# A hybrid attention, convolution and gated-MLP layer in float32: down-projection by seven block products, layer norm and output-weight splits beside the last head groups

## The chip, the cores and the metric

The kernel runs on one core of a Trainium2 chip. The time is the device time of one execution in microseconds (us). A core has five engines that run their own instruction streams and wait for each other by semaphores: TensorE (PE; PEld is its weight load), VectorE (DVE), ScalarE (ACT), GpSimd (POOL) and SyncE (SP), which here only starts transfers (DMAs).

## The reference, cut to what matters

```python
mod = silu(c) @ w_mod + b_mod                      # sh1, sc1, g1, sh2, sc2, g2
h = modulate(rms_norm(x, norm_mix_w), sh1, sc1)
proj = h @ w_in                                    # q, k, v, and the two GLU halves
attn_out = windowed_gqa_with_context(...)          # 8 query heads in 2 groups, window 128, 256 context keys
u = depthwise_conv(ga * sigmoid(gb), conv_w, conv_b)              # 31 taps, 512 channels
u = silu(layer_norm(u, conv_norm_w, conv_norm_b))                 # over the 512 channels
x = x + g1 * (concatenate([attn_out, u]) @ w_out)
h2 = modulate(rms_norm(x, norm_ffn_w), sh2, sc2)
up = depthwise_conv(h2 @ w_up, ffn_conv_w, ffn_conv_b)            # 3 taps, 2 x 2816 channels
x = x + g2 * ((silu(gate) * val) @ w_down)                        # 2816 -> 1024
```

There are 1024 latent tokens, 256 context tokens and 1024 model channels. All is float32.

## The kernel before

Products of float32 accuracy are made from three products: each operand is split into a rounded high part (ScalarE copies it to the type fp32r) and a low part (VectorE subtracts the high part), and TensorE adds high by high, high by low and low by high.

The program has two blocks. The first ends with the attention, in 16 *head groups* (`NGRP`): group n takes 128 query tokens (`i = n // 2`) and one key-value group. For each group TensorE makes scores, turns the probabilities and multiplies by the values (L639); VectorE takes the maxima (L1111, L1114) and normalises (L1187 to L1194); ScalarE takes the exponentials (L859) and moves the turned probabilities (L909). Beside groups 9 to 14 runs the layer norm of the convolution's output `cacc` (`beside(n)` on each engine): means (groups 9, 10) and variances (11, 12, L654) by matmul, the root by ScalarE, the reciprocal of `rstd` over 128x1024 by VectorE (13, 14, L1140), the scaling by GpSimd (L474). After the last group follow, one behind the other: the column sums of the second modulation (L725), its rows (L730), the SiLU of `cacc` (L928), its high and low parts (L934, L1204), and, in the second block, the splits of the eight tiles of `w_out` (L1553, L1691) before the output projection (L1440) can start. Then come the residual, the second norm and the turn of `h2`.

The up-projection (L1470) has 22 hidden tiles j of 128 channels. Each is done by a Strassen-Winograd scheme with seven block products instead of eight, in the order 1, 6, 5, 7, 2, 3, 4, twelve matmuls each. For each tile VectorE makes four sums of weight blocks (`w_sums`, L1762), seven low parts (`split_low`, L1744), five sums of products (`add`, L1833), four side taps of the convolution (`side`, L1840, L1844) and one product gate by value (L1900). The hidden tile goes to memory (`hid_scratch`).

The down-projection (L1517 to L1519) is direct: two halves of the output columns, for each half 22 hidden tiles as steps. A step is 8 token tiles by 3 matmuls, into eight accumulator banks; the operands are split per step by `down_high` and `down_low`. `drain` multiplies a half's banks by the gate `g2b` (L1915); the residual is added by GpSimd (L1944, L1951) and by VectorE (L1919). Twenty hidden tiles are loaded back from memory at the start of this stage, in six transfers (`reload`).

## Time and profile before

| | us |
|---|---|
| median of 3 runs (lowest, highest) | 1262.68 (1261.58, 1265.69) |
| the profiled execution | 1265.57 |
| its span, first to last instruction | 1263.8 |
| granted TensorE clock, mean over the span | 0.968 of full |
| TensorE busy | 1185.3 (94%) |
| VectorE busy | 882.7 (70%) |
| ScalarE busy | 523.3 (41%) |
| GpSimd busy | 131.2 (10%) |

The durations come from the profiled execution; it took 1265.57 us, 2.9 us more than the median and within the spread of the runs. Matmuls overlap, so the pace of TensorE is read from long unbroken runs, not from the duration of one.

### The profile page before, as it was taken

To read this page: it belongs to the slowest core of one execution; us is meant where nothing else is said; L and a number is where in the kernel's file an instruction comes from. 1 tells how busy PE (TensorE), PEld (TensorE's weight loads), DVE (VectorE), ACT (ScalarE), POOL (GpSimd) and SP (SyncE) were. 2 spreads that over 40 slices of the span, in tenths; PEclk is the share of its full clock that TensorE was granted. 3 is DMA by queue.
4 is the path that set the end of the run, shared out by engine and by line. 5 is a ranking of instruction groups with operands and counts; after the bars stand their busy time and mean duration, and the time that the engine had idled before them with its cause. 6 is when DMAs were issued, how large, how long until landed. Compare 5 with 4: busy or idle time off the path is not lost.

```text
span 1263.8 us, 16827 instructions
## 1 busy us (share of the span) xinstructions
PE 1185.3 (94%) x5917; PEld 979.6 (78%) x5917; DVE 882.7 (70%) x1325; ACT 523.3 (41%) x876; POOL 131.2 (10%) x140
## 2 busy tenths in 40 slices
PE   5799999898999879997899999999999999999998
PEld 1378888798978867775688888888888878887887
DVE  0479988689864634356899988888888864456445
ACT  4452356855555653544454444454454321111110
POOL 2100111044552020000000000000000000013001
PEclk9899999989999959998899999999999999999999
DMA  9222555439998005212213322322323273222112
GB/s 380 94 71 88 115 111 114 121 79 262 255 264 209 2 1 171 112 51 67 83 53 99 100 70 80 100 65 84 100 61 105 107 284 135 98 67 92 50 50 83
DMA packets 91014, 143.04 MB, mean 113 GB/s; under 512 B 7114, under 2 KB 60482, under 8 KB 89940
## 3 DMA queue, kind: packets, MB, share of 16 engines
q1 hardware_dynamic: 80292, 104.43, 24.5%
q0 software_dynamic: 9520, 33.75, 12.8%
q10 hardware_dynamic: 1152, 4.19, 0.8%
q8 instruction: 31, 0.51, 0.2%
q14 instruction: 19, 0.16, 0.0%
HBM read 96.22 MB, written 18.87 MB: 91 GB/s over the span
## 4 chain that ended last, share of the span: by engine, by line
PE 53%; DVE 5%; ACT 3%; issue 1%; DMA 1%; DVEq 0%; ACTq 0%
PE ps L1470 31%; PE ps L1517 6%; PE ps L1518 6%; PE ps L1519 6%; PE ps L1440 4%; DMA dn_raw<-in_w_down 1%; ACT h_second L1570 1%; DVE xt L1702 1%; DVE gm L1699 1%; PE ps L1451 1%; ACT gm L1557 0%; ACT h_first L1570 0%; DVE w_op L1744 0%; DVE t_sum L1733 0%; ACT hx L1574 0%
## 5 line engine op out<-in xcount | busy, mean ns | idle before, releaser
L1470 PE MATMUL ps<-t_op,w_op 128*128 128x512 f32 x1056 | 249.4, 392 | 5.8 <-DVE cv L1833 4.7
L1470 PEld LDWEIGHTS ps<-t_op,w_op 128*128 128x128 f32 x1056 | 199.6, 189 | 49.1 <-issue 4.8
L1470 PE MATMUL ps<-hx,w_op 128*128 128x512 f32 x792 | 188.9, 392 | 4.1 <-DVE p_first L1705 3.2
L1470 PEld LDWEIGHTS ps<-hx,w_op 128*128 128x128 f32 x792 | 149.5, 189 | 36.5 <-DVE p_first L1705 3.6
L1577 ACT ACTIVATE w_op<-w_raw 128x512 fp32r<-128x512 f32 x130 | 79.2, 626 | 193.2 <-DVE w_raw L1762 148.4
L1517 PE MATMUL ps<-dnh,ah 128*128 128x512 f32 x352 | 137.3, 390 | 1.3 <-DVE al L1854 1.3
L1518 PE MATMUL ps<-dnl,ah 128*128 128x512 f32 x352 | 137.0, 389 | 0.0
L1519 PE MATMUL ps<-dnh,al 128*128 128x512 f32 x352 | 137.0, 389 | 0.0
L1671 ACT ACTIVATE dnh<-dn_raw 128x512 fp32r<-128x512 f32 x44 | 27.7, 633 | 203.4 <-PE ps L1519 186.0
L1850 DVE TENSOR_SCALAR ah<-hid 128x1024 fp32r (+1 forms) x44 | 31.6, 717 | 101.0 <-PE ps L1519 101.0
L639 PE MATMUL ps<-vraw,pt 128*128 128x64 f32 x608 | 84.4, 287 | 15.8 <-ACT pt L909 15.8
L1744 DVE TENSOR_TENSOR w_op<-w_raw,w_op 128x512 fp32r<-128x512 f32 x132 | 88.9, 688 | 14.2 <-ACT w_op L1577 13.3
L639 PEld LDWEIGHTS ps<-vraw,pt 128*128 128x128 f32 x608 | 80.8, 207 | 20.8 <-ACT pt L909 10.9
L1517 PEld LDWEIGHTS ps<-dnh,ah 128*128 128x128 f32 x352 | 66.1, 188 | 16.3 <-DVE al L1854 2.6
L1440 PE MATMUL ps<-woh,hx 128*128 128x512 f32 x256 | 73.4, 404 | 5.0 <-DVE wol L1691 5.0
L1519 PEld LDWEIGHTS ps<-dnh,al 128*128 128x128 f32 x352 | 66.1, 188 | 13.9
L1518 PEld LDWEIGHTS ps<-dnl,ah 128*128 128x128 f32 x352 | 66.1, 188 | 13.5
L1111 DVE TENSOR_REDUCE scal<-ps 128x1 f32<-128x640 f32 (+1 forms) x64 | 50.2, 785 | 32.9 <-PE ps L612 27.9
L1939 POOL DMA_DIRECT2D x<-x_scratch x1 | 1.0, 1025 | 614.2 <-PE ps L1519 614.2
L859 ACT ACTIVATE p<-ps,scal,msq 128x640 f32<-128x640 f32 (+1 forms) x60 | 51.8, 863 | 26.1 <-DVE scal L1114 23.9
L1440 PEld LDWEIGHTS ps<-woh,hx 128*128 128x128 f32 x256 | 49.0, 195 | 15.6 <-DVE wol L1691 5.3
L909 ACT ACTIVATE pt<-ps 128x512 f32<-128x512 f32 x76 | 44.9, 593 | 37.1 <-PE ps L627 37.1
(265 smaller groups left out, 2228.4 us busy)
## 6 DMA issues: line engine op xcount, KB each, us to landing
w_raw<-in_w_up SPq DMA_DIRECT2D x44, 512.0 KB, 4.7
wm<-in_w_mod SPq DMA_DIRECT2D x32, 512.0 KB, 6.5
...
dn_raw<-in_w_down SPq DMA_DIRECT2D x44, 256.0 KB, 2.8
...
hid<-hid_scratch SPq DMA_DIRECT2D x4, 2048.0 KB, 12.2
...
```

The costliest lines, as they stand in the source:

```text
L639: last = pe.matmul(ps[:, 6, hl * HD:(hl + 1) * HD], pt[:, it % NPT, hl * P:(hl + 1) * P], vraw[:, kts[j], g, :], start=(j == 0 and hl == 0 ...
L859: act.activation(probs(n)[:, hl, 0:w], score_ap(hh, w), ACT.Exp, scale=msq[:, CT + n // NG, GQ * (n % NG) + hl:GQ * (n % NG) + hl + 1], bi ...
L909: act.activation(pt[:, it % NPT, :], ps[:, 4 + it % 2, :], ACT.Copy).then_inc(pt_out, 1)
L1111: dve.reduce_max(s[:, 0, hl:hl + 1], score_ap(hh, w), axis=AX.X, negate=True).then_inc(max_done, 1)
L1440: last = pe.matmul(ps[:, b + hh, :], a, (woh, wol)[lo][:, k, hh * HALF:(hh + 1) * HALF], start=(k == 0 and v == 0 and lo == 0), stop=(k == ...
L1470: last = pe.matmul(bank_of(p, s), w_op[p][w][:, k, :], rows_of(p, k, v), start=(start and k == 0 and w == 0 and v == 0), stop=(k == KH - 1 ...
L1517: pe.matmul(ps[:, t, :], ah[b][:, 0, c_], dnh[b][:], start=(kind == "first"), stop=False)
L1518: pe.matmul(ps[:, t, :], ah[b][:, 0, c_], dnl[b][:], start=False, stop=False)
L1519: return pe.matmul(ps[:, t, :], al[b][:, 0, c_], dnh[b][:], start=False, stop=(kind == "last"))
L1577: act.activation(w_op[p][0][:], w_part(s, p), ACT.Copy).then_inc(up_hi, 1)
L1744: dve.tensor_tensor(out=w_op[p][1][:], in0=w_part(s, p), in1=f(w_op[p][0][:]), op=ALU.subtract).then_inc(up_lo, 1)
L1850: dve.tensor_scalar(ah[b][:], hid[:, bass.ds(k, 1), :], 1.0, None, ALU.mult).then_inc(dn_split, 1)
```

## The change

The down-projection uses the same seven-product scheme, over blocks of 512 tokens, 512 output columns and pairs of hidden tiles. There are 77 steps (7 products by 11 pairs), each of 4 token tiles by 3 matmuls. The hidden tiles are combined in place by VectorE (`down_sum`, 44 instructions of 128x512). The combined weights are made by GpSimd while the up-projection runs: 22 chunks, each with two loads, four subtractions of 128x256 and two stores to a scratch tensor `w_down_sums`, each step waiting for the one before. Hidden tiles are loaded back one by one, at most three at a time. Operand sets are three instead of two or three, raw weight buffers four instead of two. The four output quarters are finished at different times: VectorE reads the banks (`read_quad`, 20 instructions, and 8 at the end), GpSimd multiplies by the gate and adds the residual for three quarters and prepares the fourth (28 additions or products of 128x512). The fourth quarter's last additions, on VectorE, wait for all 28.

For the layer norm, the variances come out one per token in a column (group 11), root and reciprocal are taken on 8 columns, and matmuls with a diagonal matrix (groups 13, 14) spread them; VectorE scales `cacc` from the accumulator. The SiLU runs on ScalarE inside group 15, the column sums on TensorE inside group 15, and four of the eight splits of `w_out` beside groups 13 to 15. The other four alternate with the splits of `cacc` at the start of the second block, while the projection already runs.

In the diff the pieces stand in the order layer norm (SyncE, GpSimd, TensorE, ScalarE, VectorE), then down-projection (tables, SyncE, TensorE, ScalarE, VectorE, GpSimd).

```diff
-        rstd = at(73, "rstd", [P, T])
+        diag = at(73, "diag", [P, TT, P])
+        r_ln = rst[:, 0:TT]
...
+        def wo_split_high(act, k):
+            act.wait_ge(wo_in[k % 4], 16 * (k // 4 + 1))
+            if k < KT - 1:
+                act.activation(wo_op[k][0][:].rearrange("p b n -> p (b n)"), wo_raw[:, k % 4, :], ACT.Copy).then_inc(wo_hi, 1)
...
+        def wo_split_low(dve, k):
...
+        WO_AT = {13: (0,), 14: (1, 2), 15: (3,)}
...
+                for k in range(4, KT):
+                    sp.wait_ge(wo_lo, k - 3)
+                    sp.dma_start(wo_raw[:, k % 4, :], w_out[0, k * P:(k + 1) * P, :]).then_inc(wo_in[k % 4], 16)
...
-                pool.wait_ge(rec5, 4)
-                for ct in range(CTL):
-                    pool.tensor_tensor(out=cacc[:, ct, :], in0=cacc[:, ct, :], in1=rstd[:], op=ALU.mult).then_inc(scaled, 1)
...
+                    elif n == LN + 2:
+                        pe.wait_ge(ln_act, 2 * CTL)
+                        for b in range(TT):
+                            for ct in range(CTL):
+                                last = pe.matmul(ps[:, 7, b:b + 1], sqc[ct][:, b * P:(b + 1) * P], meanw[:, 0:1], start=(ct == 0), stop=(ct == CTL - 1))
+                        last.then_inc(ln_mm, 1)
+                    elif n in (LN + 4, LN + 5):
+                        pe.wait_ge(ln_dve, 11)
+                        q = slice((n - LN - 4) * TT // 2, (n - LN - 3) * TT // 2)
+                        pe.matmul(ps[:, 7, :], ones[:], diag[:, q, :].rearrange("p b n -> p (b n)"), start=True, stop=True).then_inc(ln_mm, 1)
+                    elif n == NGRP - 1:
+                        for c in range(2):
+                            pe.wait_ge(mod_acc[1 + c], 16 * KT)
+                            for j in range(KT):
+                                last = pe.matmul(ps[:, 7, c * KT + j:c * KT + j + 1], sums[1 + c][:, j * P:(j + 1) * P], ones[:, 0:1], start=True, stop=True)
+                        last.then_inc(col_mm, 1)
...
+                        if n == NGRP - 1 and j < CTL:
+                            act.wait_ge(ln_dve, 19)
+                            act.activation(cacc[:, j, :], cacc[:, j, :], ACT.Silu, scale=cols[:, C_CNW + j:C_CNW + j + 1],
+                                           bias=cols[:, C_CNB + j:C_CNB + j + 1]).then_inc(silu5, 1)
...
+                    elif n == LN + 3:
+                        dve.wait_ge(ln_act, 9)
+                        dve.reciprocal(r_ln, r_ln).then_inc(ln_dve, 1)
+                        dve.wait_ge(ln_dve, 10)
+                        dve.tensor_tensor(out=diag[:], in0=ident[:].unsqueeze(1).to_broadcast([P, TT, P]), in1=r_ln.unsqueeze(2).to_broadcast([P, TT, P]),
+                                          op=ALU.mult).then_inc(ln_dve, 1)
                     elif n in (LN + 4, LN + 5):
-                        for r in range(2):
-                            q = slice((2 * (n - LN - 4) + r) * CTX, (2 * (n - LN - 4) + r + 1) * CTX)
-                            if n == LN + 4:
-                                dve.wait_ge(sqrt5, 1)
-                            dve.reciprocal(rstd[:, q], rstd[:, q]).then_inc(rec5, 1)
+                        hh = n - LN - 4
+                        dve.wait_ge(ln_mm, 4 + hh)
+                        for ct in range(CTL):
+                            dve.tensor_tensor(out=cacc[:, ct, half(hh)], in0=cacc[:, ct, half(hh)], in1=ps[:, 7, :], op=ALU.mult).then_inc(ln_dve, 1)
...
+        NK2 = FT // 2
+        DOWN = (1, 6, 2, 5, 7, 3, 4)
+        NSTEP = len(DOWN) * NK2
+        UPPER = (1, 2, 7, 4)
...
+            def down_rows(p, i):
+                odd, even = hid[:, 2 * i + 1, :], hid[:, 2 * i, :]
+                return {1: odd[:, 0:HALF], 6: odd[:, 0:HALF], 2: even[:, 0:HALF], 5: odd[:, HALF:T], 7: odd[:, HALF:T],
+                        3: even[:, 0:HALF], 4: even[:, HALF:T]}[p]
...
+            RELOADS = (3, 2, 21, 20, 5, 4, 7, 6, 9, 8, 11, 10, 13, 12, 15, 14, 17, 16, 19, 18)
+            FREED = {5: 6, 9: 5, 13: 7, 17: 4}
...
+                def load_step(n):
+                    p, i = down_at(n)
+                    if n >= 4:
+                        sp.wait_ge(dn_split, 2 * (n - 4) + 2)
...
+                    sp.dma_start(dn_raw[n % 4][:], src).then_inc(wo_in[n % 4], 16)
...
+                sp.wait_ge(wd_out, 32 * 2 * NK2)
...
+                for i in range(16):
+                    reload(i)
+                for i in range(16, 20):
+                    load_step(i - 12)
+                    reload(i)
+                for n in range(8, NSTEP):
+                    load_step(n)
...
+                def down_product(n, t):
+                    p, i = down_at(n)
+                    b, c_ = n % 3, slice(t * P, (t + 1) * P)
+                    o = ps[:, (4 if p in UPPER else 0) + t, :]
+                    start = i == 0 and p not in (2, 3, 4)
+                    pe.matmul(o, ah[b][:, c_], dnh[b][:], start=start, stop=False, skip_group_check=True)
+                    pe.matmul(o, ah[b][:, c_], dnl[b][:], start=False, stop=False, skip_group_check=True)
+                    return pe.matmul(o, al[b][:, c_], dnh[b][:], start=False, stop=(i == NK2 - 1), skip_group_check=True)
...
+                    act.activation(ah[n % 3][:], down_rows(p, i), ACT.Copy).then_inc(dn_hi, 1)
+                    raw_in(act, n)
+                    act.activation(dnh[n % 3][:], dn_raw[n % 4][:], ACT.Copy).then_inc(dn_hi, 1)
...
+                def down_low(n):
+                    for r, (hi, lo) in enumerate(((ah, al), (dnh, dnl))):
+                        dve.wait_ge(dn_hi, 2 * n + r + 1)
+                        src = dn_raw[n % 4][:] if r else down_rows(*down_at(n))
+                        dve.tensor_tensor(out=lo[n % 3][:], in0=src, in1=f(hi[n % 3][:]), op=ALU.subtract).then_inc(dn_split, 1)
...
+                for t in range(TT // 2):
+                    dve.wait_ge(bank_mm, t + 1)
...
+                    dve.tensor_tensor(out=gout[1][:, t, :], in0=ps[:, 4 + t, :], in1=g2b[:, 0:HALF], op=ALU.mult).then_inc(quad_read, 1)
+                    dve.wait_ge(quad_read, 20 + 2 * t + 1)
+                    dve.wait_ge(pool_step, POOL_STEPS)
+                    dve.tensor_tensor(out=gout[1][:, t, :], in0=gout[1][:, t, :], in1=p1_all[:, t, :], op=ALU.add).then_inc(quad_read, 1)
...
+                pool.wait_ge(t_lo, 4)
+                pool.wait_ge(t_sum_done, 4 * (TT // 2))
+                chunk = 0
+                for i in range(NK2):
+                    for c0 in range(0, HALF, CTX):
+                        if chunk:
+                            pool.wait_ge(wd_out, 32 * chunk)
+                        for r in range(2):
+                            k = tile_of(2 * i + 1 - r)
+                            src = w_down[0, k * P:(k + 1) * P, :].rearrange("p (g c) -> p g c", g=2)[:, :, c0:c0 + CTX]
+                            pool.dma_start(wd[r][:], src).then_inc(wd_in, 16)
+                        pool.wait_ge(wd_in, 32 * (chunk + 1))
+                        b11, b12, b21, b22 = wd[0][:, 0, :], wd[0][:, 1, :], wd[1][:, 0, :], wd[1][:, 1, :]
+                        for n, (o, a, b) in enumerate(((b11, b12, b11), (b12, b22, b12), (b22, b22, b11), (b21, b21, b22))):
+                            if chunk or n:
+                                pool.wait_ge(wd_step, 4 * chunk + n)
+                            pool.tensor_tensor(out=o, in0=a, in1=b, op=ALU.subtract).then_inc(wd_step, 1)
+                        pool.wait_ge(wd_step, 4 * chunk + 4)
+                        for r in range(2):
+                            pool.dma_start(wd_sum[2 * r:2 * r + 2, i, :, c0:c0 + CTX].rearrange("g p c -> p g c"), wd[r][:]).then_inc(wd_out, 16)
+                        chunk += 1
...
+                for t in range(TT // 2):
+                    pool.wait_ge(quad_read, 16 + t + 1)
+                    step(gout[0][:, t, :], gout[0][:, t, :], g2[1], ALU.mult)
+                    step(gout[0][:, t, :], gout[0][:, t, :], xq[0][:, t, :], ALU.add)
+                    store(t, 0, 1, gout[0][:, t, :])
+                pool.wait_ge(xq_in[1], 32)
+                for t in range(TT // 2):
+                    step(p1_all[:, t, :], u2_all[:, t, :], g2[0], ALU.mult)
+                    step(p1_all[:, t, :], p1_all[:, t, :], xq[1][:, t, :], ALU.add)
```

TensorE at the end of the head groups, before: behind the values of the last group (L639) stand the column sums (`ones,sums`, L725), the rows (L730), the turn of the last outputs (L649), then the projection (L1440).

```order
L639 MATMUL ps<-vraw,pt 128x64 x4
L627 MATMUL ps<-ident,p_103 128x128 x4
L649 MATMUL ps<-ident,on 128x128 x2
L639 MATMUL ps<-vraw,pt 128x64 x8
L725 MATMUL ps<-ones,sums_99 128x1 x8
L725 MATMUL ps<-ones,sums_100 128x1 x8
L730 MATMUL ps<-sums_98,ones 128x512 x2
L730 MATMUL ps<-sums_101,ones 128x512 x2
L649 MATMUL ps<-ident,on 128x128 x2
```

The same place now (L705 column sums, L669 values, L657 turned probabilities, L764 rows):

```order
L657 MATMUL ps<-ident,p_103 128x128 x8
L705 MATMUL ps<-ones,sums_99 128x1 x8
L705 MATMUL ps<-ones,sums_100 128x1 x8
L669 MATMUL ps<-vraw,pt 128x64 x4
L657 MATMUL ps<-ident,p_103 128x128 x4
L669 MATMUL ps<-vraw,pt 128x64 x4
L657 MATMUL ps<-ident,p_103 128x128 x4
L679 MATMUL ps<-ident,on 128x128 x2
L669 MATMUL ps<-vraw,pt 128x64 x8
L764 MATMUL ps<-sums_98,ones 128x512 x2
L764 MATMUL ps<-sums_101,ones 128x512 x2
L679 MATMUL ps<-ident,on 128x128 x2
```

The column sums have moved in front of the last group's values; only the rows and the turn of the last outputs still stand between the values and the projection.

ScalarE in group 15 and at the start of the second block, now (L950 moves probabilities, L966 is the SiLU, L305 and L308 split `w_out`, L1605 splits `cacc`, L1609 moves the gates' rows):

```order
L966 ACTIVATE cacc<-cacc,cols 128x1024
L950 ACTIVATE pt<-ps 128x512
L899 ACTIVATE hx<-ps 128x2x128
L966 ACTIVATE cacc<-cacc,cols 128x1024
L305 ACTIVATE wo_op_118<-wo_raw 128x1024
L344 UNCONDITIONAL_BRANCH
L1595 UNCONDITIONAL_BRANCH
L1600 ACTIVATE hx<-ps 128x2x128
L1605 ACTIVATE hx<-cacc 128x2x512
L305 ACTIVATE wo_op_120<-wo_raw 128x1024
L1605 ACTIVATE hx<-cacc 128x2x512
L305 ACTIVATE wo_op_122<-wo_raw 128x1024
```

Before, four SiLU, four splits of `cacc`, four moves of rows and then eight splits of `w_out` stood here in blocks behind the last group.

GpSimd during the up-projection, where nothing stood before (the scaling L474 was followed by the residual's load, L1939), now, one chunk of 22:

```order
L2066 DMA wd_5478<-in_w_down 128x2x256
L2066 DMA wd_5479<-in_w_down 128x2x256
L2072 TENSOR_TENSOR wd_5478<-wd_5478 128x256
L2072 TENSOR_TENSOR wd_5478<-wd_5479,wd_5478 128x256
L2072 TENSOR_TENSOR wd_5479<-wd_5479,wd_5478 128x256
L2072 TENSOR_TENSOR wd_5479<-wd_5479 128x256
L2075 DMA w_down_sums<-wd_5478 128x2x256
L2075 DMA w_down_sums<-wd_5479 128x2x256
```

All four subtractions have two inputs in SBUF. They run beside VectorE's work for the up-projection.

## Rows read from the trace of the kernel before

**Rows 1.** The page, part 1: busy time, share of the span, instructions

```profile
PE 1185.3 (94%) x5917; PEld 979.6 (78%) x5917; DVE 882.7 (70%) x1325; ACT 523.3 (41%) x876; POOL 131.2 (10%) x140
```

**Rows 2.** The chain of waits: start us, us, what

```profile
475.01 22.61 PE ps L1440 x90
...
634.43 381.11 PE ps L1470 x1680
...
1022.03 10.96 DMA dn_raw<-in_w_down
```

**Rows 3.** Busy time by stretch: stretch, length, engines, clock, DMA share, GB/s

```profile
450.00:475.00 25.00, 19.98 (x75) 16.12 (x73) 7.76 (x13) 16.29 (x20) 0.00 (x0) 0.57 0.00 1
634.00:1018.00 384.00, 383.73 (x1693) 317.63 (x1693) 334.50 (x442) 172.15 (x243) 0.00 (x0) 1.00 0.29 92
```

**Rows 4.** Instructions in order of time, TensorE: start us, us; in brackets idle before

```profile
441.68 1.97 PE L627 MATMUL ps<-ident,p 128*128 128x128 f32 x8 [1.81 <-ACT p L859]
447.80 1.94 PE L639 MATMUL ps<-vraw,pt 128*128 128x64 f32 x8 [4.14 <-ACT pt L909]
...
456.57 6.93 PE L725 MATMUL ps<-ones,sums 128*128 128x1 f32 x32
463.36 6.40 PE L730 MATMUL ps<-sums,ones 128*128 128x512 f32 x8
...
475.01 1.22 PE L1440 MATMUL ps<-woh,hx 128*128 128x512 f32 x2 [5.03 <-DVE wol L1691]
```

**Rows 5.** In order of time, VectorE, end of the head groups

```profile
436.52 3.35 DVE L1140 RECIPROCAL rstd<-rstd 128x256 f32<-128x256 f32 x2
...
442.28 2.35 DVE L1187 TENSOR_TENSOR scal<-scal 128x4 f32<-128x4 f32 x1
```

**Rows 6.** In order of time, GpSimd, end of the head groups

```profile
439.96 9.25 POOL L474 TENSOR_TENSOR cacc<-cacc,rstd 128x1024 f32<-128x1024 f32 x4 [43.05 <-DVE rstd L1140]
```

**Rows 7.** In order of time, ScalarE, behind the last head group

```profile
455.27 4.63 ACT L928 ACTIVATE cacc<-cacc,cols 128x1024 f32<-128x1024 f32 x4
```

**Rows 8.** In order of time, GpSimd, change of halves (second of eight alike)

```profile
1142.89 1.30 POOL L1944 TENSOR_TENSOR gout<-gout,x 128x512 f32<-128x512 f32 x1
```

**Rows 9.** In order of time, VectorE, change of halves

```profile
1139.88 0.68 DVE L1850 TENSOR_SCALAR ah<-hid 128x1024 fp32r<-128x1024 f32 x1
1140.48 2.09 DVE L1852 TENSOR_TENSOR dnl<-dn_raw,dnh 128x512 fp32r<-128x512 f32 x1
1142.49 2.79 DVE L1854 TENSOR_TENSOR al<-hid,ah 128x1024 fp32r<-128x1024 f32 x1
1145.21 1.77 DVE L1850 TENSOR_SCALAR ah<-hid 128x1024 fp32r<-128x1024 f32 x1
1146.91 2.27 DVE L1852 TENSOR_TENSOR dnl<-dn_raw,dnh 128x512 fp32r<-128x512 f32 x1
...
1151.86 0.69 DVE L1852 TENSOR_TENSOR dnl<-dn_raw,dnh 128x512 fp32r<-128x512 f32 x1
1152.47 1.22 DVE L1854 TENSOR_TENSOR al<-hid,ah 128x1024 fp32r<-128x1024 f32 x1
```

**Rows 10.** Who waited for whom, VectorE, 634 to 1010 us: total, times, longest

```profile
DVE w_op L1744 <- ACT w_op L1577: 13.3, 40, 0.7
DVE y L1840 <- ACT y L1657: 12.1, 20, 0.7
DVE u L1833 <- PE ps L1470: 8.9, 18, 0.7
```

**Rows 11.** In order of time, VectorE, inside one hidden tile

```profile
817.08 0.69 DVE L1833 TENSOR_TENSOR u<-ps,u 128x512 f32<-128x512 f32 x1 [0.59 <-PE ps L1470]
...
820.34 0.68 DVE L1833 TENSOR_TENSOR cv<-ps,u 128x512 f32<-128x512 f32 x1
```

**Rows 12.** The page, part 6: transfers, times, KB each, median us to landing

```profile
dn_raw<-in_w_down SPq DMA_DIRECT2D x44, 256.0 KB, 2.8
...
hid<-hid_scratch SPq DMA_DIRECT2D x4, 2048.0 KB, 12.2
```

**Rows 13.** In order of time, TensorE, first and last matmul of the down-projection

```profile
1018.09 0.39 PE L1517 MATMUL ps<-dnh,ah 128*128 128x512 f32 x1
...
1259.51 0.39 PE L1519 MATMUL ps<-dnh,al 128*128 128x512 f32 x1
```

541 lines of the change are left out of this document (298 added, 243 removed).

## The prediction

> **What bounds the kernel now.** I read the busy shares first, then the chain of waits, then busy time by stretch, then the waits of single engines.
>
> TensorE is busy for 94% of the span, VectorE for 70% [rows 1]. The share alone says that fewer matmuls should be worth their full price. The chain of waits says where: 1680 matmuls of the up-projection follow each other in 381.11 us without a break [rows 2], so TensorE's pace at the full clock is 381.11/1680 = 0.2268 us a matmul. In that same stretch VectorE is busy for 334.50 of 384.00 us, 87%, and GpSimd for nothing [rows 3]. That is the number to keep in mind: the stage is bound by TensorE, but VectorE is just behind it.
>
> The down-projection runs from 1018.09 to 1259.51 + 0.39 = 1259.9 us [rows 13], 241.8 us; its 1056 matmuls at 0.2268 us are 239.5, so 2.3 us are waits and starts. The rest of the span, to 1263.8, is a tail of 3.9 us.
>
> At the end of the head groups TensorE is not at its limit. It waits 1.81 and 4.14 us, then works through column sums and rows (6.93 and 6.40 us), then waits 5.03 us for the first split weights, and the projection starts at 475.01 [rows 4]. The granted clock between 450 and 475 is 0.57, so nearly all of it is at 1.2 GHz [rows 3]; it fell behind the two waits.
>
> **The change, part by part.** The sum is made against the profiled execution, 1265.6 us, which is 2.9 us above the median 1262.7. I subtract from both alike and give the time against the median.
>
> *Matmuls of the down-projection.* 77 steps x 12 = 924 instead of 1056. 132 x 0.2268 = 29.9 us less.
>
> *Start of that stage.* The steps are now 12 x 0.2268 = 2.72 us, half as long as before (24 matmuls, 5.44). VectorE's rest of the last hidden tile (side taps, gate product) covers steps 0 to 2, and splits of step 1 and of step 3 come about 1.4 and 0.9 us late: 2.5 us, as long as all waits there before (2.3). Hidden tiles: twenty of 512 KB. Before, 2048 KB landed in 12.2 us, and a weight load behind them took 10.96 us, to 1033, without a stop of TensorE [rows 12, 2]; as the reloads can't start before the last tile of the up-projection, at 1018.1 - 19.05 = 999, all 10,240 KB came in at most 34 us, 300 KB a us. With that the tiles needed by step 10 are there (by the 168 KB a us of a single transfer the last would be 15 us late); what is tight is the weights of step 4, which stand in SyncE's queue behind sixteen reloads. I take 0 for it and keep 9 us as the usual upper end.
>
> *Middle of that stage.* Per step VectorE does two low parts and at most one sum at 0.69 us [rows 9], 2.1 us and reads of banks, 2.3 of 2.72. It hides, as long as GpSimd leaves it alone.
>
> *End of that stage.* GpSimd's 28 instructions of 1.30 us [rows 8] plus about 0.3 between dependent ones. In the last product 8 of them wait for VectorE's reads at steps 1, 3, 5 and 7, the last at about 15.7 us, and 8 more follow: 15.7 + 4.1 + 8 x 1.6 + 5 for the port (below) = 37.6 us after that product's start, while TensorE needs 29.9 + 2.5 (VectorE's splits held up by those instructions) = 32.4. Then 7 VectorE instructions of 0.69 and a store of 2 us: the end is at about 45, where TensorE's end plus the old tail would be 33.8. That is 11 to 12 us lost, of which the tail is most. Together the down-projection gives 29.9 - 0.2 - 12 = 17.7; I take 18, range 8 to 24.
>
> *Layer norm and output weights.* Off the path behind the last group go: the column sums (6.93 us there, half of that at the full clock inside group 15), SiLU (4.63 us for four [rows 7]), the splits of `cacc`, and the wait of 5.03. What makes the 4.14 us wait goes too: GpSimd's scaling of 128x1024 (9.25 us for four [rows 6]) held a VectorE instruction on four elements for 2.35 us, and the two reciprocals before it took 3.35 [rows 5]; now four products of 0.69 us stand in their place. Added inside groups 13 to 15: two spreading matmuls (about 0.9 us each, by eight instructions of 128x512 at half clock in 6.40 us), four splits of 1.06 and 1.23 us, SiLU with its table between the moves of probabilities. The last values end, I estimate, at 449 instead of 456.6; the rows take 3.2 at full and 6.4 at half clock; first projection at about 454. That is 21 us earlier than 475.01. The first two token tiles take 22.61 us [rows 2] against 96 x 0.2268 = 21.8. The remaining splits (VectorE 2.5 us a tile, TensorE 2.72 a tile) keep ahead. I take 21 us, range 10 to 25.
>
> *GpSimd beside the up-projection.* This is the term that decides. A GpSimd subtraction of 128x512 takes 1.30 us [rows 8], one of 128x1024 9.25/4 = 2.31 [rows 6]; 1.01 us per 512 columns and 0.29 fixed, so 0.80 us for 128x256. What does it cost VectorE? At the change of halves four VectorE instructions took 2.09 + 2.79 + 1.77 + 2.27 = 8.92 us against 0.69 + 1.22 + 0.68 + 0.69 = 3.28 undisturbed [rows 9]: 5.64 us more, for four GpSimd instructions of 1.30 us, 1.08 times their length. The two engines take turns. Per hidden tile of 84 x 0.2268 = 19.05 us VectorE has 16 instructions with two SBUF inputs, 11 of 128x512 at 0.69 and 5 of 128x1024 at 1.22 [rows 9], 13.7 us or 0.72; those that read the accumulators are not held. So one subtraction costs 0.80 x 1.08 x 0.72 = 0.62 us and 88 of them 55 us. From this goes VectorE's slack. Its waits are 13.3, 12.1 and 8.9 us over twenty tiles [rows 10]; the 12.1 and a quarter of the 13.3 are its own chains through ScalarE and stay, the other 19 us are about 1.0 to 1.1 a tile. A chunk is two loads (3.4 us with 2.8 to landing [rows 12]), four subtractions with turns taken (6) and two stores (3.5), 13 us; 22 chunks last 286 us, 14 tiles, 15 us of slack. Once, a lead is used up: the sum `cv` is made at 820.34 to 821.0, and product 4 needs it three products of 2.72 us after 817.08 [rows 11], at 825.2, 4 us later. So TensorE loses 55 - 15 - 4 = 36 us. Bounds: no less than 0 (nothing VectorE does gets faster); with 0.80 x 1.08 = 0.86 us each, held every time, 76 - 19 = 57. I take 36.
>
> The Trainium skill (GPSIMD Engine Reference, section 3.1, "side-by-side cycle accounting") gives 4497 ns for a two-input addition of 2048 columns. Estimated from that page alone, 256 columns take 0.56 us, the term becomes 88 x 0.56 x 1.08 x 0.72 - 19 = 19 us and the whole time 1243. Rows 6 and 8 show a fixed part of 0.29 us on top, which such a short instruction pays in full, so I go by the rows.
>
> Sum: -18 - 21 + 36 = -3; 1262.7 - 3 = 1260 us (1262 to 1263 for a profiled execution like the one read here).
>
> **Rivals.**
> *B. The weight sums are nearly hidden.* If GpSimd mostly gets in while VectorE waits or reads accumulators, or its turns are short, one subtraction costs 0.3 us: 26 - 19 = 7. Time 1262.7 - 39 + 7 = 1231. For it: TensorE has leads of 4 us and more, and VectorE has waits in each tile. Against: rows 9, where no turn was cheap.
> *C. VectorE becomes the bound of the up-projection for good, and it is slower.* Each subtraction is held or holds for its full 0.86 us: 57. Time 1262.7 - 39 + 57 = 1281. It decides from (39 + 19)/88 = 0.66 us each, only 6% above my value. For it: the turn costs a running VectorE instruction too, and waits of TensorE of 2 us and more came before the fall of its clock [rows 4, 3]. The Trainium skill (GPSIMD Engine Reference, section 1) says that GpSimd's SBUF interfaces contend with VectorE instructions "in a 2-port perf mode or with two SBUF inputs", which is the same list. The trace agrees: the reads of accumulators beside GpSimd kept 0.69 us.
> *D. The head groups give back only half.* ScalarE's table load, SiLU and splits stand between the moves of probabilities that TensorE waits for; 10 instead of 21: 1270.
>
> **How the numbers follow.** Forecast 0.50, B 0.22, C 0.20, D 0.08. A measurement of this kernel tells about 0.3%, 3.8 us, from no change. Around 1260 with some 8 us either way, the forecast divides into 0.23 faster, 0.16 same, 0.11 slower. B adds 0.22 to faster; C and most of D (0.27) to slower, 0.01 to same. So faster 0.45, same 0.17, slower 0.38. The forecast's own range is 1249 to 1271. Both signs hold much of the chance, so the range must reach to B and to C: 1232 to 1284.
>
> **What would show it.** In the profile after: in the stretch of GpSimd's chunks the period of a hidden tile, 22 to 23 us in the forecast, 19.5 in B, over 24 in C; TensorE's waits there named VectorE's `cv` or `w_op`; VectorE's low parts at 1.5 us beside a subtraction and 0.69 otherwise; a subtraction of 128x256 at 0.80 us. First projection matmul at about 454 us (D: 465). First to last matmul of the down-projection about 215 us, and a tail of about 12 us with VectorE waiting for GpSimd. Wrong is the prediction if the up-projection keeps its 381 us per twenty tiles, or if the down-projection stops for hidden tiles or weights for more than 5 us.

## The result, and the profile after

The changed kernel takes 1246.13 us, median of 4 runs (1244.12 to 1248.26), beside 1262.86 us (1261.58 to 1265.69) for the kernel before: a ratio of 0.9882, 95% interval 0.9858 to 0.9907. It is 1.2% faster. The forecast was 1260 us, the range 1232 to 1284. The profiled execution took 1244.66 us, with a span of 1242.9; before it was 1265.57 and 1263.8.

Here the difference of the two spans is split at the first matmul of a stage. The output projection's start stands in [rows 4], the down-projection's in [rows 13]; the up-projection of the kernel before began at 582.4.

| us | before | after | difference | predicted |
|---|---|---|---|---|
| first matmul of the output projection | 475.0 | 462.0 | -13.0 | -21 |
| first matmul of the up-projection | 582.4 | 566.8 | -15.6 | (same term) |
| up-projection | 435.7 | 445.8 | +10.1 | +36 |
| down-projection, first to last matmul | 241.8 | 224.7 | -17.1 | -27 |
| tail behind it | 3.9 | 5.6 | +1.7 | +8 |
| span | 1263.8 | 1242.9 | -20.9 | -3 |

Two terms of the sum of -3 were somewhat too good (head groups -21 against -15.6, down-projection with its tail -18 against -15.4), and one was much too bad: +36 against +10.1. The spans differ by 20.9 us and the medians by 16.7: the two traces lie 4.2 us further apart, and the trace of before has a spell at the half clock of about that price that the other has not (below).

Busy time of the changed kernel (the line that answers to [rows 1]):

```profile
PE 1158.3 (93%) x5837; PEld 958.3 (77%) x5837; DVE 945.7 (76%) x1405; ACT 579.1 (47%) x991; POOL 317.0 (26%) x335
```

The stretches that answer to [rows 3], columns as there:

```profile
450.00:475.00 25.00, 24.35 (x97) 19.32 (x98) 11.89 (x15) 16.26 (x22) 0.00 (x0) 0.82 0.16 54
634.00:1012.00 378.00, 375.33 (x1646) 307.78 (x1645) 346.18 (x428) 159.73 (x233) 140.85 (x152) 1.00 0.45 145
```

TensorE made 1693 matmuls in 384 us before, 4.409 a us; now 1646 in 378, 4.354. Its clock is full (1.00) in both. Count the matmuls rather than the busy time: the 1.2% that is missing is short waits. By this pace a hidden tile of 84 matmuls takes 19.3 us, against 19.05 before, 22 to 23 in the forecast and 19.5 in rival B.

**The head groups.** TensorE in order of time, from group 9 on (the third row and those below answer to [rows 4]), with idle time before in brackets:

```profile
356.55 3.60 PE L689 MATMUL ps<-cacc,meanw 128*128 128x512 f32 x8
...
387.46 10.77 PE L695 MATMUL ps<-meanw,sqc 128*128 128x1 f32 x64
...
443.86 3.63 PE L705 MATMUL ps<-ones,sums 128*128 128x1 f32 x32
...
450.33 1.97 PE L669 MATMUL ps<-vraw,pt 128*128 128x64 f32 x8 [1.29 <-ACT pt L950]
...
453.37 3.52 PE L669 MATMUL ps<-vraw,pt 128*128 128x64 f32 x16
456.68 4.75 PE L764 MATMUL ps<-sums,ones 128*128 128x512 f32 x8
461.26 0.38 PE L679 MATMUL ps<-ident,on 128*128 128x128 f32 x2
461.97 19.32 PE L1483 MATMUL ps<-wo_op,hx 128*128 128x512 f32 x84 [0.32 <-PEq L344]
```

The waits of 4.14 and 5.03 us and the 6.93 us of column sums behind the last group are gone, as predicted. Yet the rows L764 begin at 456.68, where the column sums began at 456.57 before; the prediction had the last values end at 449. So nothing was won inside the groups, and the dearest new piece there is the second line: the variance is now made in columns, 32 products of one column each (two records a product). They take 10.77 us, and VectorE stands still behind them:

```profile
401.78 0.82 DVE L1142 TENSOR_REDUCE scal<-ps 128x1 f32<-128x640 f32 x1 [13.46 <-PE ps L642]
```

In the kernel before, the variance was two wide sets, and the means of group 9 stood here:

```profile
360.66 3.60 PE L654 MATMUL ps<-cacc,meanw 128*128 128x512 f32 x8
391.55 3.60 PE L654 MATMUL ps<-sqc,meanw 128*128 128x512 f32 x8
405.80 3.60 PE L654 MATMUL ps<-sqc,meanw 128*128 128x512 f32 x8
```

Two things follow. The columns themselves cost 3.6 us more than the 7.2 of the two sets; the rest of their price is the half clock that TensorE had behind them, to 407 (from 385 to 415 the mean granted clock is 0.72, before it was 1.00). And the changed kernel was already 4.1 us ahead in group 9, before anything that the change moved: between 310 and 320 us the granted clock was 0.76 before and 1.00 after, over the same instructions. Of the 13.0 us only about 9 belong to the change.

**The up-projection.** GpSimd's subtractions, least, middle and longest time in ns:

```profile
L2072 POOL TENSOR_TENSOR wd<-wd x44: 726/1034/1714, 598.2 to 909.5; 128x256 f32<-128x256 f32 x44
L2072 POOL TENSOR_TENSOR wd<-wd,wd x44: 732/1076/1715, 599.1 to 907.8; 128x256 f32<-128x256 f32 x44
```

The shortest took 0.73 us (I had 0.80 for an undisturbed one); the median is 1.03 to 1.08. So here GpSimd waits for its turn too. TensorE's longest waits from 565 us to the end, in total, times and longest:

```profile
PE ps L1568 <- DVE dnl L1928: 10.1, 4, 5.1
PE ps L1518 <- DVE cv L1910: 7.9, 7, 6.4
PE ps L1518 <- DVE p_first L1782: 4.2, 1, 4.2
PE ps L1518 <- DVE u L1910: 3.7, 4, 2.3
```

VectorE's own waits, 634 to 1005 us, answer to [rows 10]: the slack was spent first.

```profile
DVE w_op L1821 <- ACT w_op L1633: 6.9, 37, 0.5
DVE y L1917 <- ACT y L1713: 6.6, 14, 0.7
...
DVE u L1910 <- PE ps L1518: 1.2, 2, 0.7
```

**The down-projection.** First and last matmul (as [rows 13]), then the chain of waits into its fifth step:

```profile
1012.59 0.39 PE L1568 MATMUL ps<-dnh,ah 128*128 128x512 f32 x1
...
1236.93 0.39 PE L1570 MATMUL ps<-dnh,al 128*128 128x512 f32 x1
```

```profile
1014.86 8.11 DMA hid<-hid_scratch
1022.99 0.33 SPq L1450
1023.36 6.14 DMA dn_raw<-in_w_down
1029.53 0.64 ACT dnh L1735
1030.19 0.70 DVE dnl L1928
1030.94 0.80 PE ps L1568
```

The transfer of the weights of step 4 is issued at 1023.36, behind sixteen reloads, before which SyncE waits for earlier ones to land (at most three are on their way). It takes 6.14 us, against a median of 2.8 before [rows 12], and lands at 1029.50, and TensorE, which had waited 5.12 us, goes on at 1030.94. The eleven matmuls behind it come every 0.43 us instead of 0.23: the granted clock is at 1.2 GHz until 1035.6.

At the other end, VectorE beside GpSimd's last eight instructions (VectorE, then GpSimd):

```profile
1222.55 2.26 DVE L1928 TENSOR_TENSOR al<-hid,ah 128x512 fp32r<-128x512 f32 x1
1224.74 1.78 DVE L1928 TENSOR_TENSOR dnl<-dn_raw,dnh 128x512 fp32r<-128x512 f32 x1
1226.45 1.74 DVE L1928 TENSOR_TENSOR al<-hid,ah 128x512 fp32r<-128x512 f32 x1
1228.11 1.74 DVE L1928 TENSOR_TENSOR dnl<-dn_raw,dnh 128x512 fp32r<-128x512 f32 x1
...
1235.18 0.69 DVE L2052 TENSOR_TENSOR gout<-gout,p_all 128x512 f32<-128x512 f32 x1 [1.79 <-POOL p_all L2089]
```

```profile
1222.96 1.30 POOL L2089 TENSOR_TENSOR p_all<-u_all,g2b 128x512 f32<-128x512 f32 x1
...
1233.78 1.30 POOL L2089 TENSOR_TENSOR p_all<-p_all,xq 128x512 f32<-128x512 f32 x1
```

Low parts of 0.69 us take 1.74 to 2.26, and TensorE stands for 3.40 us before its last two steps (matmul at 1230.01).

### The profile page after: what moved, and what is told of

The parts are those of the page before. It is cut to its first block, busy times and chain, and to the rows that moved or that the text cites. A ratio compares the mean times of both kernels' runs of the same rounds, so it can differ in the third digit from the quotient of the medians.

```text
span 1242.9 us, 16857 instructions
## 1 busy us (share of the span) xinstructions
PE 1158.3 (93%) x5837; PEld 958.3 (77%) x5837; DVE 945.7 (76%) x1405; ACT 579.1 (47%) x991; POOL 317.0 (26%) x335
## 4 chain that ended last, share of the span: by engine, by line
PE 32%; DVE 15%; issue 6%; ACT 6%; DMA 3%; DVEq 0%; ACTq 0%; SPq 0%
PE ps L1518 13%; PE ps L1568 5%; PE ps L1569 5%; PE ps L1570 5%; PE ps L1483 3%; DVE w_op L1821 3%; DVE y L1921 3%; DMA hid<-hid_scratch 2%; DVE w_raw L1839 2%; ACT w_op L1633 1%; DVE y L1917 1%; ACT y L1713 1%; DVE u L1910 1%; DVE s_sum L1839 1%; ACT h_second L1626 1%
## 5 line engine op out<-in xcount | busy, mean ns | idle before, releaser
L1568 PE MATMUL ps<-dnh,ah 128*128 128x512 f32 x308 | 121.9, 396 | 10.1 <-DVE dnl L1928 10.1
L1569 PE MATMUL ps<-dnl,ah 128*128 128x512 f32 x308 | 121.5, 395 | 0.0
L1570 PE MATMUL ps<-dnh,al 128*128 128x512 f32 x308 | 121.3, 394 | 0.0
L1733 ACT ACTIVATE ah<-hid 128x512 fp32r<-128x512 f32 x77 | 48.6, 632 | 113.3 <-PE ps L1570 104.8
L2066 POOL DMA_DIRECT2D wd<-in_w_down x44 | 32.0, 729 | 271.8 <-DVE h_first L1810 199.3
L669 PE MATMUL ps<-vraw,pt 128*128 128x64 f32 x608 | 84.2, 287 | 8.9 <-ACT pt L950 8.9
L1928 DVE TENSOR_TENSOR al<-hid,ah 128x512 fp32r<-128x512 f32 x77 | 63.6, 826 | 36.0 <-ACT ah L1733 35.1
L669 PEld LDWEIGHTS ps<-vraw,pt 128*128 128x128 f32 x608 | 80.3, 206 | 13.6 <-ACT pt L950 10.6
L1483 PE MATMUL ps<-wo_op,hx 128*128 128x512 f32 x336 | 80.2, 395 | 0.3 <-PEq L344 0.3
L1483 PEld LDWEIGHTS ps<-wo_op,hx 128*128 128x128 f32 x336 | 62.9, 190 | 13.7 <-issue 0.5
L1928 DVE TENSOR_TENSOR dnl<-dn_raw,dnh 128x512 fp32r<-128x512 f32 x77 | 68.0, 884 | 6.4 <-ACT dnh L1735 6.2
L2072 POOL TENSOR_TENSOR wd<-wd 128x256 f32<-128x256 f32 x44 | 46.2, 1051 | 71.5 <-DMA wd<-in_w_down 69.8
```

The lines of the kernel that those rows point to most:

```text
L669: last = pe.matmul(ps[:, 6, hl * HD:(hl + 1) * HD], pt[:, it % NPT, hl * P:(hl + 1) * P], vraw[:, kts[j], g, :], start=(j == 0 and hl == 0 ...
L1483: last = pe.matmul(ps[:, b + hh, :], a, wo_half(k, lo, hh), start=(k == 0 and v == 0 and lo == 0), stop=(k == KT - 1 and v == 1))
L1568: pe.matmul(o, ah[b][:, c_], dnh[b][:], start=start, stop=False, skip_group_check=True)
L1569: pe.matmul(o, ah[b][:, c_], dnl[b][:], start=False, stop=False, skip_group_check=True)
L1570: return pe.matmul(o, al[b][:, c_], dnh[b][:], start=False, stop=(i == NK2 - 1), skip_group_check=True)
L1733: act.activation(ah[n % 3][:], down_rows(p, i), ACT.Copy).then_inc(dn_hi, 1)
```

## Experiments

All are edits of the changed kernel; each was run beside the kernel before, so ratios are the means of comparison. A stage's length is more exact than the whole time: the eight kernels with identical head groups begin their projection at 459.8 to 466.3 us, 72.8 to 78.7 us after the first product of the variance. Where nothing in them differs, the up-projection takes 444.3 to 446.7 us and the down-projection 224.2 to 227.9; its wait for the weights of step 4 is 5.1 to 8.6 us.

### 1 and 2. What costs the up-projection its 10 us

The first leaves out the subtractions:

```diff
-                        for n, (o, a, b) in enumerate(((b11, b12, b11), (b12, b22, b12), (b22, b22, b11), (b21, b21, b22))):
...
-                            pool.tensor_tensor(out=o, in0=a, in1=b, op=ALU.subtract).then_inc(wd_step, 1)
```

The second leaves out the whole loop over chunks, and the down-projection loads unchanged weights in their place:

```diff
-                        src = wd_sum[{5: 0, 7: 1, 4: 2, 6: 3}[p], i]
+                        src = w_down[0, k * P:(k + 1) * P, 0:HALF]
...
-                for i in range(NK2):
-                    for c0 in range(0, HALF, CTX):
...
```

> The changed kernel without GpSimd's four subtractions per chunk beside the up-projection; the chunks' loads and stores stay (the weights of four products are then not combined: the computation is incomplete). Theory (the turns that GpSimd and VectorE take at SBUF cost the whole loss of the up-projection): the stage, 445.8 us in the changed kernel, falls by 8 to 11 us to about 436, the 6.4 us stop of TensorE near 605 shrinks to 4 to 5, VectorE's low parts of weights go from 811 back to about 690 ns; time about 1236 us. Rival (the chunks' 88 transfers beside the stage's own are the cost): the stage stays above 443 us, time above 1243.

> The changed kernel without the chunks at all: neither loads, nor subtractions, nor stores beside the up-projection; the down-projection loads unchanged weights of the same size in their place (the computation is incomplete). Theory (turns of the two engines only): the same as the kernel without subtractions, within 1 us in the up-projection, about 436 us. Rival (transfers): only here does the stage come back to 436, and the kernel without subtractions stays in between or above 443.

Measured: without subtractions 1239.58 us, ratio 0.9835 (0.9789 to 0.9882), up-projection 436.7 us. Without chunks 1237.69, ratio 0.9830 (0.9788 to 0.9872), up-projection 436.7 us. Shown: the transfers cost nothing, the subtractions 9.1 us. The last 1.0 us of the 10.1 is in both: TensorE's wait for `p_first`, 4.2 us in all three kernels, was 3.2 before. The stretch from 700 to 800 us, changed kernel, without subtractions, without chunks:

```profile
700.00:800.00 100.00, 98.90 (x434) 80.78 (x433) 93.73 (x114) 43.56 (x65) 52.09 (x56) 1.00 0.47 152
```
```profile
700.00:800.00 100.00, 100.00 (x443) 82.84 (x442) 87.67 (x116) 45.42 (x64) 29.93 (x42) 1.00 0.55 187
```
```profile
700.00:800.00 100.00, 100.00 (x443) 82.81 (x442) 87.75 (x115) 44.15 (x63) 0.00 (x0) 1.00 0.30 89
```

This gives the price of one. For 434 matmuls VectorE needs 87.67 x 434/443 = 85.89 us; it was busy for 93.73, 7.84 more, and 28 subtractions lie in the stretch: 0.28 us each. 88 of them are 24.6 us, of which 9.1 reached TensorE; the other 15.5 were slack.

### 3. Twice as many subtractions

```diff
                             pool.tensor_tensor(out=o, in0=a, in1=b, op=ALU.subtract).then_inc(wd_step, 1)
+                        for n, (o, a, b) in enumerate(((b11, b12, b11), (b12, b22, b12), (b22, b22, b11), (b21, b21, b22))):
+                            pool.wait_ge(wd_step, 8 * chunk + 4 + n)
+                            pool.tensor_tensor(out=o, in0=a, in1=b, op=ALU.subtract).then_inc(wd_step, 1)
```

> The changed kernel with every subtraction of GpSimd's chunks done twice, 176 instead of 88 (the combined weights are then wrong). If what a subtraction costs is always 10.1/88 = 0.11 us net, the up-projection grows by about 10 us to 456. My theory has VectorE's slack in between: a subtraction holds VectorE for 0.31 us, 27 us in all, of which 17 were slack that the second set no longer finds; 27 more with no slack left are +20 to +30 us in the stage, 466 to 476, less what falls past its end because chunks are then longer (about 19 instead of 14 us, 22 of them 420 us, still inside). The prediction's size, 0.62 us each, would give +55.

Measured: 1288.97 us, ratio 1.0220 (1.0177 to 1.0263); up-projection 468.8 us, 23.0 more than in the changed kernel. In the same stretch:

```profile
700.00:800.00 100.00, 96.39 (x414) 76.63 (x413) 94.57 (x110) 40.66 (x60) 66.30 (x60) 1.00 0.41 131
```

By the same working, 94.57 - 87.67 x 414/443 = 12.64 us for 40 subtractions, 0.32 each, and 176 of them 56 us, of which 32.1 reached TensorE. The first 88 lost 9.1, the second 23.0: the loss is the held time less a slack. The slack is 23.9 us here, because the chunks last longer: one begins every 19.9 us instead of 14.6, which by itself makes 21. The last subtraction now ends at 1030.6 and its stores are issued behind it, which I had not expected, so the down-projection, too, waits for its weights (242.8 us).

### 4. The output weights' splits behind the groups again

```diff
-        WO_AT = {13: (0,), 14: (1, 2), 15: (3,)}
+        WO_AT = {}
...
                 output_high(NGRP - 1)
+                for k in range(CTL):
+                    wo_split_high(act, k)
...
                 output_low(NGRP - 1)
+                for k in range(CTL):
+                    wo_split_low(dve, k)
```

> The changed kernel with the four splits of output weights that were moved into the last head groups put back behind them, ScalarE's and VectorE's, right after the last group's output; the loads of the others behind them. Theory (those splits are what spared the wait of 5.03 us before the first projection): first projection 2 to 4 us later than 461.97 and the first two token tiles, 20.7 us now, a further 2 to 6 us longer, since the engines have splits of the weights and of cacc one after another; time 4 to 9 us above the changed kernel. Rival (the splits in the groups cost as much as they spare, because they stand before moves of probabilities): within 2 us.

Measured: 1252.13 us, ratio 0.9908 (0.9873 to 0.9943), against 0.9882: inconclusive as a whole. In the trace the wait is back, 2.94 us, and the projection begins 3.3 us later than in the changed kernel; 1.5 us of these were there at the variance:

```profile
461.92 0.38 PE L676 MATMUL ps<-ident,on 128*128 128x128 f32 x2
465.25 7.08 PE L1483 MATMUL ps<-wo_op,hx 128*128 128x512 f32 x30 [2.94 <-DVE wo_op L315]
```

So these splits were worth about 3 us, read from one wait and not clear of the spread of the whole time. The further 2 to 6 us that I expected in the first two token tiles did not come: TensorE has no second wait there.

### 5. The variance's columns in fp32r

```diff
-        sqc = [at(kib, f"sqc{ct}", [P, T]) for ct, kib in enumerate((99, 103, 139, 77))]
+        sqc = [at(kib, f"sqc{ct}", [P, T], F32R) for ct, kib in enumerate((99, 103, 139, 77))]
...
-                                last = pe.matmul(ps[:, 7, b:b + 1], sqc[ct][:, b * P:(b + 1) * P], meanw[:, 0:1], start=(ct == 0), stop=(ct == CTL - 1))
+                                last = pe.matmul(ps[:, 7, 2 * b:2 * b + 2], sqc[ct][:, b * P:(b + 1) * P], meanr[:], start=(ct == 0), stop=(ct == CTL - 1))
```

> The changed kernel with the variance's 32 column products of the layer norm (128x1 each, fp32, 10.77 us at 387.46) done in fp32r with two equal columns. Theory (these columns, and the fall of the clock behind them, are where the head groups lost what the prediction counted on): they take 3 to 4 us, the head groups end 6 to 9 us earlier, first projection at 453 to 456, as the prediction had it; time 6 to 9 us below the changed kernel. Rival (TensorE's later waits for ScalarE and VectorE in groups 12 to 15 take up what is gained): first projection above 459, less than 3 us.

Measured: 1240.29 us, ratio 0.9831 (0.9795 to 0.9867), some 6 us below the changed kernel (the two intervals overlap a little; the trace is clearer).

```profile
387.98 3.95 PE L696 MATMUL ps<-meanr,sqc 128*128 128x2 f32 x32
```
```profile
455.80 16.37 PE L1486 MATMUL ps<-wo_op,hx 128*128 128x512 f32 x71 [0.32 <-PEq L345]
```

3.95 us instead of 10.77, and the first projection at 455.8, where the prediction had 454. From the first product of the variance to the projection it is 67.8 us, and 66.2 in experiment 11, which has the same edit, against 72.8 to 78.7 in the eight kernels without it. The granted clock of the stretch 400 to 430 is 0.97 here and 0.73 to 0.95 in those eight. The theory holds.

### 6. SiLU behind the groups again

```diff
-                        if n == NGRP - 1 and j < CTL:
-                            act.wait_ge(ln_dve, 19)
-                            act.activation(cacc[:, j, :], cacc[:, j, :], ACT.Silu, scale=cols[:, C_CNW + j:C_CNW + j + 1],
...
                     beside(n)
...
+                for j in range(CTL):
+                    act.wait_ge(ln_dve, 19)
+                    act.activation(cacc[:, j, :], cacc[:, j, :], ACT.Silu, scale=cols[:, C_CNW + j:C_CNW + j + 1],
...
```

> The changed kernel with the four SiLUs, and the table load before them, put behind the last group's moves of probabilities again. Theory (rival D of the prediction on a small scale: the table load makes TensorE wait 1.29 us at 450.33 and its clock falls to 1.2 GHz until the projection): that wait goes, the last values end 1 to 3 us earlier, the rows take 3.2 instead of 4.75 us, first projection 3 to 6 us earlier, and the splits of cacc, needed only at the fifth step of a token tile, stay hidden; time 2 to 5 us less. Rival: the last output's high part now waits behind SiLU on ScalarE (6 us), and with it the second token tile; time 0 to 4 us more.

Measured: 1247.47 us, ratio 0.9878 (0.9844 to 0.9913): no difference that its interval would show. The wait of 1.29 us is gone and the splits of `cacc` stay hidden, but nothing was won: in this execution, the slowest of the six, the clock had fallen before, in the column sums, and stayed down.

```profile
449.91 4.83 PE L705 MATMUL ps<-ones,sums 128*128 128x1 f32 x32
454.61 1.95 PE L669 MATMUL ps<-vraw,pt 128*128 128x64 f32 x8
```

In this execution the first projection came at 468.8, but 3 us of that were there at the variance (390.4 instead of 387.5), and from 400 to 430 the clock was 0.70. So no run shows a cost of the SiLU inside the groups, rival D's cause; one of up to 4 us would not be seen in the whole time. What sets the moment of the clock's fall stays open.

### 7. The weights of step 4 earlier

```diff
-                for i in range(16):
+                steps_after = {8: 4, 11: 5, 13: 6, 16: 7, 18: 8}
+                for i in range(20):
                     reload(i)
-                for i in range(16, 20):
-                    load_step(i - 12)
-                    reload(i)
...
+                    if i in steps_after:
+                        load_step(steps_after[i])
...
+                pool.wait_ge(dn_mm, NK2)
                 load_quad(0, 0, 0)
```

> The changed kernel with the weights of steps 4 to 8 of the down-projection put earlier in SyncE's queue (behind reloads 8, 11, 13, 16 and 18 instead of behind 16 and later), and GpSimd's first two residual loads of 2 MB held back until the first eight steps are done. Theory (the wait of 5.12 us at 1030.94 is for the weights of step 4, which the prediction took as 0): that wait goes, and the half clock behind it; the stage falls by 6 to 9 us. Rival (the stage's transfers are at their limit, about 400 GB/s from 998 to 1030, so a hidden tile comes too late instead): TensorE waits as long for a reloaded tile some steps later; 0 to 2 us.

Measured: 1237.45 us, ratio 0.9830 (0.9789 to 0.9870); down-projection 217.4 us, 7.3 less. SyncE's issues:

```profile
995.99 12.01 SPq L1450 DMA_DIRECT2D hid<-hid_scratch  x9
1008.04 0.51 SPq L1442 DMA_DIRECT2D dn_raw<-in_w_down  x1
```

The only waits left at the start are 1.09 and 0.51 us, and no hidden tile comes late. Both edits were made together, so how much the held residual loads give is open; with the unchanged stage at 224.2 to 227.9 us, 6.8 us is the least that the two give.

### 8 and 9. GpSimd's last eight instructions

In the first (8) they follow directly on the first quadrant's; the second (9) has the two waits as well. In both, VectorE's last additions wait for the first 12 of GpSimd's 28 instructions only:

```diff
-        POOL_STEPS = 28
+        POOL_STEPS = 12
...
                     store(t, 0, 0, gout[0][:, t, :])
-                load_quad(0, 0, 1)
+                load_quad(0, 1, 1)
+                pool.wait_ge(xq_in[1], 16)
+                for t in range(TT // 2):
+                    pool.wait_ge(dn_mm, NK2 * DOWN.index(7) + 2 * t + 1)
+                    step(p1_all[:, t, :], u2_all[:, t, :], g2[0], ALU.mult)
+                    pool.wait_ge(dn_mm, NK2 * DOWN.index(7) + 2 * t + 2)
+                    step(p1_all[:, t, :], p1_all[:, t, :], xq[1][:, t, :], ALU.add)
+                load_quad(1, 0, 1)
```

> The changed kernel with GpSimd's eight instructions on the last quadrant (the gate and the residual for what the last product is added to) done right after the first quadrant's instead of last. Theory (GpSimd's instructions beside the last product's splits make TensorE wait about 4.5 us near 1225, and the last of them hold VectorE 1.79 us at 1235.18): eight fewer instructions beside the last product, tail 5.6 to 4 us; 3 to 6 us less. Rival (the same instructions cost the same waits beside product 5 or 7): 0 to 2 us.

> As the kernel with the last quadrant's eight GpSimd instructions done earlier, but one of them at a time, each behind a step of product 7 (where VectorE has two splits a step and no sum, 1.4 of 2.72 us and the reads). Theory (a GpSimd instruction of 128x512 takes VectorE about 1.1 us per split that it meets; done back to back they fill VectorE for 12 us, and TensorE waits wherever that falls; spread over steps with slack they cost nothing): no stop in product 7, none of the 3.4 us before the last two steps, VectorE's 1.79 us wait for GpSimd gone; last product to last matmul and tail 4 to 6 us shorter than in the changed kernel. Rival (it isn't a matter of the density but of their number): the loss stays within 2 us of the changed kernel's, as in the kernel before this.

Measured: done early but in a row, 1245.02 us, ratio 0.9878 (0.9837 to 0.9919), nothing gained, where 3 to 6 us were expected; spread, 1240.73 us, ratio 0.9820 (0.9781 to 0.9859). In the first, VectorE fills up where the eight now stand, and TensorE loses there what it won at the end:

```profile
1120.00:1150.00 30.00, 25.53 (x109) 20.12 (x108) 29.27 (x28) 10.40 (x19) 20.80 (x16) 0.99 0.43 132
```

That is 109 matmuls instead of some 132 at the rate of [rows 3]. Spread over steps of 2.72 us with two low parts and no sum, each meets one low part, which takes 1.23 us for 0.68:

```profile
1160.71 1.23 DVE L1928 TENSOR_TENSOR al<-hid,ah 128x512 fp32r<-128x512 f32 x1 [0.29 <-ACT ah L1733]
```

The GpSimd instruction of this pair is the first below. The two lines under it are another pair of the same trace, from the first quadrant, whose four GpSimd instructions stand 5.7 us apart:

```profile
1160.09 1.30 POOL L2089 TENSOR_TENSOR p_all<-p_all,xq 128x512 f32<-128x512 f32 x1 [1.42 <-PE ps L1570]
...
1126.04 1.66 POOL L2089 TENSOR_TENSOR gout<-gout,xq 128x512 f32<-128x512 f32 x1 [3.16 <-DVE gout L2014]
1126.47 1.78 DVE L1928 TENSOR_TENSOR dnl<-dn_raw,dnh 128x512 fp32r<-128x512 f32 x1
```

Though they stand alone, those cost VectorE 1.10 us each and not 0.55. In both pairs the loss is a little less than what was left of GpSimd's instruction when VectorE's began: 0.55 us of 0.68, 1.10 of 1.23.

TensorE has no wait at all from 1035 us to its last matmul; down-projection 220.7 us, though its wait for the weights of step 4 was 6.7 instead of 5.12; tail 4.3. The same eight instructions cost about 5 us or nothing, by where they stand.

### 10. The chunks spread

```diff
+                        pool.wait_ge(prod, 21 + 11 * chunk // 2)
                         for r in range(2):
```

> The changed kernel with GpSimd's 22 chunks of weight sums begun one every 5.5 products (about 15.5 us) from the fourth hidden tile on, in place of one after another from the second. Theory (what is lost is VectorE's time beyond its slack, and the slack is that of all tiles, while the first two tiles have none: TensorE stopped there for 6.40 us against 4.44 without subtractions, and 2.26): the up-projection falls from 445.8 to 438 to 442 us; time 4 to 8 us less. Rival (each subtraction costs its 0.1 us net wherever it stands): 444 to 447.

Measured: 1246.21 us, ratio 0.9867 (0.9832 to 0.9902); up-projection 443.7 us, 2.1 less than in the changed kernel and 7.0 more than without subtractions. TensorE's stop near 605 went back from 6.40 to 4.45 us, as expected, and that is the whole of the gain: the rest stayed. Both forecasts missed, the rival's by 0.3 us. The first loads of the first and of the last chunk were issued at 644.51 and 963.67, before at 593.76 and 900.87: a chunk every 15.2 us instead of 14.6, which is only 4% more slack, 0.6 us. I had counted the slack of all tiles without working out how little more of it the spacing reaches. The theory survives, the gain does not. The time didn't move at all because the down-projection took 227.9 us here, its wait for the weights of step 4 being 8.6 us.

### 11. Four edits together (5, 7, 9, 10)

> The changed kernel with four edits together: the variance's columns in fp32r, the weights of steps 4 to 8 earlier in SyncE's queue, the last quadrant's GpSimd instructions spread over product 7, the chunks of weight sums spread over the tiles from the fourth on. If the places are independent the gains add: 6 + 7 + 5 + 6 = 24 us, time 1222, range 1216 to 1230. Rival (one gain eats another: what comes earlier waits at the next place, above all the start of the down-projection): 1231 to 1236.

Measured: 1225.68 us, median of 6 (1218.02 to 1227.38), ratio 0.9702 (0.9665 to 0.9739) to the kernel before: 3.0% faster than it, and 1.8% faster than the changed kernel (0.9702/0.9882 = 0.982). By the single ratios (0.9831, 0.9830, 0.9820, 0.9867 against 0.9882) the gains are 6.4, 6.6, 7.8 and 1.9 us, 22.7 in all; together they gave (0.9882 - 0.9702) x 1262 = 22.7. Each ratio is known to about 0.004, 5 us, so the exact agreement is luck, but within that they add, and the rival's 1231 to 1236 is out. In the profiled execution, the fastest of the six, what TensorE still waits for on VectorE from the up-projection on is mostly old (4.7 us on `cv` before, 6.6 now):

```profile
PE ps L1521 <- DVE cv L1913: 6.6, 8, 4.4
...
PE ps L1571 <- DVE dnl L1931: 2.4, 3, 1.1
```

## Why the prediction was right in its direction and wrong in its size

The sum of -3 was what +36 and -39 left, and the chances stood at 0.45 for faster and 0.38 for slower: the direction was hardly forecast. The distance of 14 us from the median, too, is smaller than the error of one term (26 us too bad), since head groups (5.4) and down-projection (2.6) were too good and the two traces lie 4.2 us further apart than the medians. That the time fell inside the range is due to a range of 52 us.

*Matmuls of the down-projection, -29.9.* Right: 924 at 0.2268 us are 209.6, and the stage is that and its waits.

*Start of that stage, taken as 2.5 us with the weights of step 4 at 0.* This failed, near the upper end of 9 that was kept for it. The small waits were 1.09 and 0.51 us; the wait for step 4 was 5.12 and the low clock behind it about 2 more; putting the weights earlier gave back 7.3. The prediction had said that it would be wrong if this stage stopped for weights for more than 5 us, and by that sign this term was. I had named the queue behind which the load stands and then priced it by the transfers' total rate, as if the last tile needed first were what mattered.

*End of that stage, 11 to 12 us lost.* The mechanism was right, the place was not. The last eight GpSimd instructions ran from 1222.96 to 1235.08, 33.1 us after their product's start (TensorE stopped at 1226.6 after 108 of its matmuls, so it began at about 1202) and not 37.6: the 5 us that I added to GpSimd for the port were VectorE's to pay. So the tail grew by 1.7 us only, and TensorE waited 3.40 us before its last steps instead. Experiment 9 puts the whole at about 5 us.

*Layer norm and splits, -21, measured -13.0 at the first projection and -15.6 at its end.* The step that failed is "added inside groups 13 to 15": the list left out group 11, where the variance changed from wide products to single columns. Experiment 5 gives back 6.2 us of the 8 with that one change, and comes to 455.8. That this is so near the predicted 454 is partly luck: 4.1 us of it are the lead in group 9, which the change did not make. Measured from the variance on, the changed kernel won 9 us of the 21, experiment 5 another 7, and some 5 stay unexplained. The splits in the groups were worth about 3 us.

*GpSimd beside the up-projection, +36, measured +10.1 (9.1 by experiment 1).* The frame held: held time, less a slack (15 us and a lead of 4 in the prediction, 15.5 found by experiment 1). The size did not: 0.28 us a subtraction, not 0.62, near rival B's 0.3. This is the term that was mis-sized most. I took the ratio 1.08 of held time to GpSimd's length from [rows 9], where GpSimd ran its instructions one behind the other against VectorE's unbroken splits, and where it is nearly true now: 1222.55 to 1229.9, four low parts took 7.52 us instead of 2.76, 4.8 more, beside four GpSimd instructions of 1.3 to 1.6. Beside the up-projection GpSimd waited too: a subtraction took 1.03 to 1.08 us for 0.73. Experiment 9 shows two more values, 0.55 and 1.10 us for instructions that stand alone. How densely the two engines work can't alone set the price, then. What fits is that VectorE loses nearly what is left of GpSimd's instruction when its own begins, and GpSimd the same the other way round, so that it costs most when both run without a gap. Beside the up-projection the remainders from 700 to 800 us add up to 10.6 us for the 28 subtractions, 0.38 each, of which 0.28 were lost. No run varied the remainder alone.

From the figure of the Trainium skill (GPSIMD Engine Reference, section 3.1, side-by-side cycle accounting) I had estimated 0.56 us for 256 columns; the shortest of the 88 took 0.726. So the fixed part was real, and yet the estimate from the page, 1243 us, came nearer to the result, by luck: the error lay in the other factor. What section 1 (Specifications) of the same page of the Trainium skill says, that GpSimd contends with VectorE's instructions with two SBUF inputs, is borne out by experiments 1 to 3.

*Rivals.* B's mechanism came true, with its 7 us against 10.1, but its time of 1231 did not, since the subtractions cost 3 us more, the head groups and the down-projection 8, and the traces lie 4 us further apart than the medians. C would have needed 0.66 us each. D had the right size in the head groups: 10 us, and 9 are the change's own. No run bears out its cause: the SiLU between the moves of probabilities cost nothing that experiment 6 can show, and the splits there gave 3 us in experiment 4; experiment 5 shows another cause.
